# Query products of the retrieval layer for both token tiles at once, in one-pass form, with GpSimd making low parts

## The reference, cut to what matters

```python
qh = (xt @ w_query).reshape(T, PEER_HEADS, PEER_KEY_DIM)          # 8 heads, 256 wide
s1 = jnp.einsum('thd,nd->thn', qh[..., :half], sub_keys_1)        # 128 scores
s2 = jnp.einsum('thd,nd->thn', qh[..., half:], sub_keys_2)
v1, i1 = lax.top_k(s1, PEER_TOPK); v2, i2 = lax.top_k(s2, PEER_TOPK)   # 16 each
cand = v1[..., :, None] + v2[..., None, :]                        # best 16 of the sums
top_s, top_j = lax.top_k(cand.reshape(..., 256), PEER_TOPK)
gate = softmax(top_s)
a = gelu(xc . expert_u[ec]);  y = (gate * a) @ expert_v[ec]       # 128 experts a token
```

## Time and profile before

| | us |
|---|---|
| median of 3 runs | 991.89 |
| lowest, highest | 991.84, 993.48 |
| the profiled execution | 992.11 |
| its span in the profile | 990.3 |
| busy: TensorE, its weight loads | 974.4, 870.2 |
| busy: VectorE, ScalarE, GpSimd | 761.6, 531.3, 312.0 |

### The profile page before, as it was taken

One profiled execution on the slowest core, in us unless ns is written; L12 is line 12 of the kernel. 1 busy time (PEld: TensorE's weight loads), 2 busy tenths in 40 slices (PEclk: granted clock), 3 DMA queues, 4 the chain that ended last, 5 costly groups with the idle time before them and its releaser, 6 DMA issues.

```text
span 990.3 us, 17661 instructions
## 1 busy us (share of the span) xinstructions
PE 974.4 (98%) x6306; PEld 870.2 (88%) x6306; DVE 761.6 (77%) x1879; ACT 531.3 (54%) x1121; POOL 312.0 (32%) x370
## 2 busy tenths in 40 slices
PE   9999999999999999999999999999999999999996
PEld 4888866999999999999999999988888888888885
DVE  4577635799898888889999999666666666666668
ACT  3555522234446888888888887433333333333341
POOL 1000000000220999999999998000000000000000
PEclk9999999999999999999999999999999999999998
DMA  9383202873555454454454454766555556555551
GB/s 328 140 349 129 107 2 77 264 298 109 189 177 171 166 171 160 161 164 163 164 170 155 167 166 155 252 237 192 192 190 195 193 192 200 191 199 190 192 171 42
DMA packets 48807, 176.52 MB, mean 178 GB/s; under 512 B 5185, under 2 KB 6225, under 8 KB 47569
## 3 DMA queue, kind: packets, MB, share of 16 engines
q1 hardware_dynamic: 48320, 173.82, 51.8%
q0 software_dynamic: 400, 1.58, 0.5%
HBM read 174.33 MB, written 1.05 MB: 177 GB/s over the span
## 4 chain that ended last, share of the span: by engine, by line
PE 88%; DVE 7%; DMA 2%; ACT 1%; issue 1%; SPq 1%; DVEq 0%
PE ps L488 86%; DMA arena<-in_w_tok 2%; DVE lo L1560 1%; PE ps L681 1%; DVE pair L1748 1%; DVE arena L1693 1%; DVE hi L1560 1%; DVE arena L1698 1%; DVE arena L1701 0%; ACT hi L1077 0%; SPq L386 0%; DVE slab L1758 0%; DVE arena L1762 0%; DVE xs L1837 0%; DVE xs L1831 0%
## 5 line engine op out<-in xcount | busy, mean ns | idle before, releaser
L488 PE MATMUL ps<-x1hl,hi 128*128 128x256 f32 x2248 | 374.2, 283 | 0.6 <-DVE hi L1560 0.6
L488 PEld LDWEIGHTS ps<-x1hl,hi 128*128 128x128 f32 x2248 | 330.4, 192 | 0.9 <-DVE hi L1560 0.8
L488 PE MATMUL ps<-hi,ahl 128*128 128x512 f32 x992 | 265.3, 389 | 0.0
L1248 ACT CAST hi<-slab 128x1024 fp32r<-128x1024 f32 x128 | 135.3, 1057 | 204.5 <-PE ps L488 204.5
L488 PE MATMUL ps<-x1hl,lo 128*128 128x256 f32 x824 | 233.2, 283 | 0.0
L488 PEld LDWEIGHTS ps<-hi,ahl 128*128 128x128 f32 x992 | 186.1, 188 | 38.6
L470 POOL TENSOR_SCALAR hot<-slab 128x128 fp32r<-128x128 f32 x224 | 197.6, 896 | 0.0
L488 PEld LDWEIGHTS ps<-x1hl,lo 128*128 128x128 f32 x824 | 158.2, 192 | 0.0
L1781 DVE TENSOR_TENSOR lo<-slab,hi 128x1024 fp32r<-128x1024 f32 x128 | 156.0, 1219 | 0.0
L488 PE MATMUL ps<-lo,ahl 128*128 128x512 f32 x496 | 152.6, 389 | 0.0
L1560 DVE TENSOR_TENSOR lo<-slab,hi 128x1024 fp32r<-128x1024 f32 x97 | 122.0, 1258 | 18.9 <-ACT hi L1077 18.5
(11 more groups left out here) (209 smaller groups left out, 1014.9 us busy)
## 6 DMA issues: line engine op xcount, KB each, us to landing
slab<-in_uT SPq DMA_DIRECT2D x128, 512.0 KB, 3.3
slab<-in_pv SPq DMA_DIRECT2D x128, 512.0 KB, 4.1
arena<-in_wq SPq DMA_DIRECT2D x32, 512.0 KB, 5.1
arena<-in_w_tok SPq DMA_DIRECT2D x8, 512.0 KB, 9.6
arena<-in_w_out SPq DMA_DIRECT2D x1, 4096.0 KB, 15.6
arena<-in_w_tok SPq DMA_DIRECT2D x1, 2048.0 KB, 15.6
arena<-in_w_tok SPq DMA_DIRECT2D x1, 1792.0 KB, 19.0
slab<-in_xT SPq DMA_DIRECT2D x4, 256.0 KB, 7.6
```

Of the source, the lines that this page charges most:

```text
L488: return nc.tensor.matmul(o, lhsT, rhs, start=start, stop=stop, skip_group_check=True)
L1248: nc.scalar.copy(hi[:, v_hi_slot(c), :], raw[:, v_slot(c), :]).then_inc(v_hi, 1)
```

## The change

Eleven of the sixteen query blocks (5 to 15) are made for both tiles at once, as three one-pass products with 256 columns instead of two float32 products with 128. The 32 steps become 21: blocks 0 to 4 of tile 0 alone, 5 to 15 for both, 0 to 4 of tile 1 alone (`STEPS`; `ALONE` = 5).

- ScalarE makes the high parts of the eleven weight blocks (`split_query`): five right after tile 0's turned copy, ahead of the first `save_query`, and one behind each of the steps 5 to 10. GpSimd makes the low parts, in place in the ring. The ring has ten places instead of seven (three `more`), and blocks 7 to 9 are loaded once the last attention product is done.
- Tile 1 is turned before step 4 instead of before step 14. Its high part is copied by ScalarE from PSUM (`high_x1`), its low part made by VectorE from PSUM (`low_x1`), and ScalarE keeps a full copy for the single blocks (`keep_x1`). Step 5 waits for both tiles' parts.
- VectorE ranks four pairs of tile 1 between those of tile 0, before `topped`; the other four come after `route(0)`.
- The first group stands before block 36 instead of 33, the last before 125 instead of 123; the turn of the routing result before block 33. 32 rests are made inside the routing, at other counts; GpSimd makes those of blocks 26 and 29 too.

```diff
-N0 = 33
-NROUTE = 29
-NTURN = 30
-FILL_AT = (54, 55, 57, 66, 68, 68, 76, 79, 79, 86, 89, 89, 97, 99, 99, 106, 109, 109, 119, 120, 120, 123, 124,
-           124, 127, 128, 129, 130, 131,)
+N0 = 36
+NROUTE = 32
+NTURN = 33
+FILL_AT = (59, 61, 72, 73, 74, 74, 77, 78, 78, 81, 82, 82, 85, 86, 86, 93, 96, 96, 103, 106, 106, 119, 120,
+           120, 123, 124, 124, 127, 128, 128, 130, 131,)
-POOL_LOW = range(5, 26, 3)
-GROUP_AT = [N0 + g * (123 - N0) // 63 for g in range(GN)]
+POOL_LOW = range(5, 32, 3)
+GROUP_AT = [N0 + g * (125 - N0) // 63 for g in range(GN)]
+ALONE = 5
+A_WQH, WQH = A_EQ, 5
+A_MORE, MORE = A_WQH + WQH * D, 3
+STEPS = ([(0, j) for j in range(ALONE)] + [(T, j) for j in range(ALONE, 2 * PH)]
+         + [(1, j) for j in range(ALONE)])
-FIRST_HI = (22, 23, 26)
+FIRST_HI = (18, 19, 21)
...
+            def load_query(n):
+                if n >= RING + MORE:
+                    sp.wait_ge(pe_q, n - RING - MORE + 1)
+                elif n >= RING:
+                    sp.wait_ge(pe_pv, NU)
+                sp.dma_start(query_raw(n), wq[STEPS[n][1]]).then_inc(query_here(n)[0], 16)
...
+            for n in range(ALONE, 2 * PH):
+                pool.wait_ge(q_hi, n - ALONE + 1)
+                nc.gpsimd.tensor_tensor(query_low(n), query_raw(n),
+                                        wq_hi[:, n % WQH, :].bitcast(F32), ALU.subtract).then_inc(q_lo, 1)
...
+            def query(n):
+                who, j = STEPS[n]
...
+                if n == ALONE:
+                    pe.wait_ge(x1_split, 2 * T)
+                if n == 2 * PH:
+                    pe.wait_ge(x1_kept, 2)
+                pe.wait_ge(*query_here(n))
+                if who == T:
+                    pe.wait_ge(q_lo, n - ALONE + 1)
+                if n >= 2:
+                    pe.wait_ge(q_saved, n - 1)
+                w, w_high, w_low = query_raw(n), wq_hi[:, n % WQH, :], query_low(n)
                 for k in range(KD):
+                    ks = slice(k * P, (k + 1) * P)
+                    if who < T:
+                        last = mm(ps[:, 4 + n % 2, 0:P], w[:, ks], x1T[who][:, k, :], k == 0, k == KD - 1)
+                    else:
+                        for m, (a, part) in enumerate(((w_high, 0), (w_high, 1), (w_low, 0))):
+                            last = mm(ps[:, 4 + n % 2, 0:S], a[:, ks], x1hl[:, k, part, :], k == 0 and m == 0,
+                                      k == KD - 1 and m == 2)
...
-                if j == 2 * PH - 2:
+                if n == ALONE - 1:
                     turn_x1(1)
...
+            for n in range(ALONE, ALONE + WQH):
+                split_query(n)
+            for n in range(len(STEPS)):
+                if n in FIRST_HI:
+                    u_split(FIRST_HI.index(n))
+                save_query(n)
+                if n == 0:
+                    root(1)
+                if n == ALONE - 2:
+                    high_x1()
+                    keep_x1()
+                if ALONE + WQH <= n + WQH < 2 * PH:
+                    split_query(n + WQH)
...
+            def low_x1():
+                for part in range(2):
+                    ks = slice(4 * part, 4 * part + 4)
+                    dve.wait_ge(pT_saved, nth("x", 1, part) + 1)
+                    v.tensor_tensor(x1hl[:, ks, 1, P:S], ps[:, 6 + part, :].rearrange("p (k n) -> p k n", k=4),
+                                    x1hl[:, ks, 0, P:S].bitcast(F32), ALU.subtract).then_inc(x1_split, 1)
...
-            split_x1(0)
-            for b in range(0, 10, 2):
+            split_x1()
+            low_x1()
+            for b in range(0, ALONE, 2):
                 subkey_tops(0, b)
...
-            for b in range(10, 2 * PH, 2):
+            for b in range(ALONE + ALONE % 2, 2 * PH, 2):
                 subkey_tops(0, b)
-            split_x1(1)
+                if b + 2 < 2 * PH:
+                    subkey_tops(1, b)
             settle()
             v.tensor_scalar(lnst[:, 0, 6:7], lnst[:, 0, 7:8], 0.0, None, ALU.add).then_inc(topped, 1)
             route(0)
-            for b in range(0, 2 * PH, 2):
+            for b in (2 * PH - 2, *range(0, ALONE, 2)):
                 subkey_tops(1, b)
             route(1)
```

More of the change, by code:

```diff
@@ L132 @@
 A_V = A_ALL - 1024
+ALONE = 5
+A_WQH, WQH = A_EQ, 5
+A_MORE, MORE = A_WQH + WQH * D, 3
+assert A_MORE + MORE * D <= A_WMQ
+STEPS = ([(0, j) for j in range(ALONE)] + [(T, j) for j in range(ALONE, 2 * PH)]
+         + [(1, j) for j in range(ALONE)])
+SCORED = [(t, j) for who, j in STEPS for t in range(T) if who in (t, T)]
 ALL4, PAIRS, EVEN, ODD = (0, 1, 2, 3), ((0, 1), (2, 3)), (0, 2), (1, 3)
@@ L298, in peer_layer_kernel @@
         l_w1, l_w2, l_wo, l_ln1 = sem("l_w1"), sem("l_w2"), sem("l_wo"), sem("l_ln1")
-        l_ring = [sem(f"l_ring{b}") for b in range(RING)]
+        l_ring = [sem(f"l_ring{b}") for b in range(RING + MORE)]
         l_sk, l_ln2 = sem("l_sk"), sem("l_ln2")
@@ L369, in pool_lows, with query_raw, query_low, query_here @@
             return sum(b <= c for b in POOL_LOW)
+        def query_raw(n):
+            b = n % (RING + MORE)
+            return ring[:, b, :] if b < RING else more[:, b - RING, :]
+        def query_low(n):
+            b = n % (RING + MORE)
+            return ring_lo[:, b, :] if b < RING else more_lo[:, b - RING, :]
+        def query_here(n):
+            return l_ring[n % (RING + MORE)], (n // (RING + MORE) + 1) * 16
         def v_slot(c):
@@ L419, in _ @@
             sp.dma_start(xs[:, 1, :], x[:, 1, :]).then_inc(l_x, 16)
-            for j in range(RING, 22):
-                load_query(j)
+            for n in range(RING, len(STEPS) - 4):
+                load_query(n)
             sp.wait_ge(pe_mix, 2 * T)
@@ L425, in _ @@
                 load_u(c)
-            for j in range(22, 28):
-                load_query(j)
+            for n in range(len(STEPS) - 4, len(STEPS)):
+                load_query(n)
             sp.wait_ge(topped, 1)
@@ L430, in _ @@
                 load_u(c)
-            for j in range(28, 4 * PH):
-                load_query(j)
             for c in range(UR, NK):
@@ L752, in turn_x1, with subkey_scores @@
                     last.then_inc(pe_pT, 1)
[L754 to L762, removed]
+            def subkey_scores(n):
+                who, j = STEPS[n]
+                pe.wait_ge(q_saved, n + 1)
+                if n >= 1:
+                    pe.wait_ge(sk_saved, sum(2 if w == T else 1 for w, _ in STEPS[:n]))
+                for i in range(2 if who == T else 1):
+                    last = mm(ps[:, 3, i * P:(i + 1) * P], qT[:, n % 2, i * P:(i + 1) * P], subk_sb[:, j % 2, :], True, True)
+                last.then_inc(pe_sk, 1)
@@ L773, in query @@
                 last.then_inc(pe_q, 1)
-                if j >= 1:
-                    subkey_scores(j - 1)
+                if n >= 1:
+                    subkey_scores(n - 1)
             pe.wait_ge(warm_zero, 1)
@@ L894, in _ @@
             advance(mix1, 4)
-            for j in range(4 * PH):
-                if j == 2 * PH - 2:
+            for n in range(len(STEPS)):
+                if n == ALONE - 1:
                     turn_x1(1)
-                query(j)
-            subkey_scores(4 * PH - 1)
+                query(n)
+            subkey_scores(len(STEPS) - 1)
             def expert_in(c):
@@ L1586, in subkey_tops @@
             def subkey_tops(t, b):
-                dve.wait_ge(sk_saved, 2 * PH * t + b + 2)
+                dve.wait_ge(sk_saved, max(SCORED.index((t, i)) for i in (b, b + 1)) + 1)
                 top16([(V[:, t, i, :], IX[:, t, i, :], sc[t][:, i, :]) for i in (b, b + 1)])
```

85 lines of the change are left out of this document (49 added, 36 removed).

## The result

The changed kernel takes 998.33 us (median of 6 runs, 995.47 to 999.35), the kernel before 992.59 us beside it (6 runs, 991.76 to 993.48). The ratio is 1.0056, with a 95% interval of 1.0043 to 1.0069: 5.7 us slower by the medians, where 2.6 were forecast. The profiled execution took 998.93 us around a span of 997.1.

What follows compares the result with a forecast made beforehand. The prediction took TensorE as the bound, with VectorE's routing exactly on time and without slack. It summed -3.0 (routing's end) + 5.3 (extra holds) + 0.3 (groups) to +2.6 us, 994.5 us, range 985 to 999.

Steps and rivals of the forecast that it cites:

- Term 1: Query and score products: eleven shared blocks replace 22 single ones, saving TensorE 7.6 us (7.0 to 8.4).
- Term 2: Second tile's normalisation: VectorE is held by GpSimd's five subtractions, so query(5) starts 2.8 us late.
- rival (c): Normalisation and routing: GpSimd wins the turns and more holds are full, 2.5 + 3 us more, 1000 us; chance 0.09.
- Rival (b): Normalisation: the port costs nothing at the start either, -7.6 us, 984.3 us; chance 0.12.
- The clock: TensorE's granted clock: 1.00 in all the stretches read, including a 0.58 us wait, so nothing was put on it.
- Term 3: Routing: its end moves by -3.0 us, and eight holds at 1.05 us make 8.4, 5.3 more than before.
- Term 4: Groups: 63 steps over 89 blocks instead of 90 cost +0.3 us, between 0 and 1.5.
- (a): Routing: the holds are fewer, giving 989.2 us with as much hold as before or 987.1 with none; chance 0.24.

Runs made afterwards that it cites:

- e4: Changed kernel with GpSimd's subtractions of nine expert and eleven query blocks cut to 8 columns, their low parts left out of the result: 983.54 us, ratio 0.9910.
- e9: Changed kernel with GpSimd waiting until the first tile's x1 is split, and the candidates' codes and compared list moved to PSUM: 984.26 us, ratio 0.9909.
- e6: Changed kernel with GpSimd waiting until the first tile's x1 is split, and thirteen rests on GpSimd at other blocks instead of nine: 985.86 us, ratio 0.9935.
- e7: Changed kernel with GpSimd waiting until the first tile's x1 is split, and fifteen rests on GpSimd at other blocks instead of nine: 985.40 us, ratio 0.9927.
- e1: Changed kernel with one added wait: GpSimd makes no query low part until VectorE has split the first tile's x1: 991.74 us, ratio 0.9995.
- e12: The kernel of e9 with the last group before block 126 instead of 125: 987.30 us, ratio 0.9959.

## Why the prediction was wrong where it was

The sign and the mechanism were right (slower, by the shared access in the normalisation and in the routing); the size was 2.6 us against 5.7.

**Term 1** (7.6 us saved): 7.35 between two kernels without the port's cost, and shared blocks at 3.32 us. Right. (Its upper bound, 8.4, does not come out of 0.1195 us for a product; that makes 7.8.)

**Term 2** (2.8 us lost before the first shared block) is the step that failed. It measured 7.0: 4.6 from holds and 2.4 from half clock. The step read that "this takes VectorE's next instruction to win against a waiting GpSimd", from one pair of rows in the gate stage. In the normalisation they take turns strictly: all four instructions stood behind a subtraction, as rival (c) had it for this place (5.3 against 4.6 for the holds; the cast and L1623 came out free, since GpSimd's five subtractions were over by 174.6). Rival (b), that such instructions are not held, fell with the same rows: L1605 and L1614 are SCALAR_TENSOR_TENSOR. Why VectorE won twice running at 588.9 and never here stays open.

**The clock**, which I put at nothing because no wait of before had touched it, is the other half of the same step. The waits that I knew of were 0.58 us. A term that makes a wait of 4 us goes beyond what those rows can say, and I forecast a start near 177 without asking what the clock would do in between.

**Term 3** (holds of 8.4 us in the routing) had the holds too small and the time right, and that is partly luck. They measured 12.2 us in seven meetings instead of eight at 1.05. I took the mean of a few hits and misses; the real ones are longer, since VectorE's own rests wait for the same copies of ScalarE that release GpSimd's and so start at its side (255.97 and 255.89). Yet the routing from `topped` to the start of the rest of block 32 takes 102.8 us (224.76 to 327.55), where 97.0 + 5.3 = 102.3 were forecast. Without the holds it takes 94.3 (e4, 217.76 to 312.05), so they cost 8.5 of their 12.2 us; the others fell largely where VectorE would have stood anyway: its waits for ScalarE's copies are 3.3 us in e4 and 0.4 in the changed kernel. I had not counted those waits. `topped` itself came at 224.76 instead of 220.9, by the lateness of Term 2. TensorE's waits were 5.6 us, and the second half-clock stretch cost some 1.7 (half of 3.41, an estimate): 7.3 against 7.1 forecast. Together: 7.35 saved, 7.0 lost before the first shared block, 7.3 lost in the routing, about +7.0, near the 6.8 between the spans.

**Term 4** (+0.3 for the groups) measured nothing: 0.6 us of waits against 1.15. The two runs on it show that the last block is not free to move by itself: 2.5 and 3.0 us in the kernel of e9.

Rivals (a) and (b), with 0.36 between them, needed GpSimd's subtractions to meet little; e4, e6, e7 and e9 show that such a kernel exists (983.5 to 985.9, beside their 984.3 and 987 to 989), but not with the work where the change puts it.

## What to carry to other kernels

Before work is handed to GpSimd, list what VectorE does in each window of it: beside MAX8, FIND_INDEX8, reduces and two-input instructions with an operand in PSUM it cost nothing in these runs, beside SBUF-only two-input instructions, casts and TENSOR_SCALAR it costs up to its own length, and on a path that TensorE waits for it costs more than that. One added wait took back the loss (e1), and with one operand moved to PSUM as well a change that lost 5.7 us gains 8 (e9). Where a forecast contains a new wait of TensorE of some microseconds, give the clock a term.

## What the runs showed of the hardware beyond expectation

- In the normalisation GpSimd and VectorE alternated instruction by instruction, both wanting the shared access: 1.78, 2.83, 2.64 and 2.82 us for four VectorE instructions of 0.75, and 2.8 instead of 2.4 us for GpSimd's beside them. In the gate stage of before VectorE went twice running, and in e9 GpSimd was the one held, by a rest that started 0.06 us behind it.
- A CAST and a TENSOR_SCALAR of 0.22 us with one SBUF input were held 2.2 and 2.1 us. A TENSOR_TENSOR of 128x1600 with one operand in PSUM was not held (1.81 us, 3.51 with both in SBUF).
- A wait of TensorE of 4.00 us was followed by 6.83 us at half clock in the changed kernel and in the run without rests, and by 3.41 us in the one with the rests on VectorE; a wait of 1.89 us by 3.41 us in one execution and by none in two; and beside a wait of 2.52 us in e12 stand 3.41 us. What decides between these is open; it was not tried further.
